# Attention in a two-layer hybrid network: probabilities scaled on GpSimd, latent attention in groups of two head columns

## The reference, cut to what matters

```
s = (q @ k.T) * scale                 # in C2: q,k of 64 columns, plus 32 rope columns whose k is shared by all heads
p = softmax(where(mask, s, NEG))      # B2: a window of 128 and a sink logit in the sum; D2: an added bias
o = p @ v
NSA: out = g0 * o_compressed + g1 * o_selected + g2 * o_window     # gates per token and head
```

## Time and profile before

| | us |
|---|---|
| median of 3 runs | 2278.95 |
| lowest, highest | 2278.51, 2280.58 |
| span of the profiled execution | 2275.0 |
| own time of the profiled execution | not listed apart from its span; the median is 3.95 above the span |
| TensorE busy in the span | 2199.9 |
| VectorE busy | 1246.9 |
| ScalarE busy | 1078.0 |
| GpSimd busy | 853.7 |

### The profile page before, as it was taken

The page is one execution under the profiler, slowest core; times in us unless marked ns, Lnnn a source line. Parts: engine busy times, 40 slices in busy tenths (PEclk is TensorE's granted clock), DMA queues, the critical chain, the costliest instruction groups (busy, mean ns, idle before and its releaser), DMA issues.

```text
span 2275.0 us, 33281 instructions
## 1 busy us (share of the span) xinstructions
PE 2199.9 (97%) x12130; PEld 1763.7 (78%) x12130; DVE 1246.9 (55%) x2614; ACT 1078.0 (47%) x2160; POOL 853.7 (38%) x665
## 2 busy tenths in 40 slices
PE   8999899999999999989999999999999999999997
PEld 6778667888866788668888888888767888888886
DVE  6997782499778446885552112234666655211222
ACT  6542484465247652685453223343566545322332
POOL 4333304443330343104255545554110425554553
PEclk9999899999999999999999999999999999999998
DMA  5334002332410233203233333343110323333331
GB/s 171 85 91 141 25 2 79 104 91 79 144 38 11 75 89 109 68 2 110 67 94 96 95 109 98 92 124 95 48 60 20 111 66 97 94 95 100 98 96 66
DMA packets 107186, 189.74 MB, mean 83 GB/s; under 512 B 12049, under 2 KB 22801, under 8 KB 106897
## 3 DMA queue, kind: packets, MB, share of 16 engines
q1 hardware_dynamic: 101136, 178.67, 27.3%
q10 hardware_dynamic: 5888, 8.95, 1.2%
HBM read 182.85 MB, written 2.10 MB: 81 GB/s over the span
## 4 chain that ended last, share of the span: by engine, by line
PE 85%; DVE 10%; issue 3%; ACT 2%; POOL 1%; DMA 0%; SPq 0%; DVEq 0%; ACTq 0%
PE bank L861 23%; PE bank L863 23%; PE bank L862 23%; PE bank L1090 3%; PE bank L1103 3%; PE bank L1076 2%; DVE temp L1933 1%; DVE bank L2053 1%; PE bank L868 1%; DVE temp L1965 1%; PE bank L1067 1%; PE bank L1070 1%; PE bank L931 1%; DVE temp L1967 1%; POOL w_lo L2212 1%
## 5 line engine op out<-in xcount | busy, mean ns | idle before, releaser
L2212 POOL TENSOR_TENSOR w_lo<-w_raw,w_hi 128x512 fp32r<-128x512 f32 (+3 forms) x618 | 824.7, 1341 | 1337.1 <-ACT w_hi L1226 1336.7
L861 PE MATMUL bank<-op_hi,w_hi 128*128 128x512 f32 x1840 | 734.4, 399 | 9.1 <-POOL w_lo L2212 4.4
L863 PE MATMUL bank<-op_hi,w_lo 128*128 128x512 f32 x1840 | 719.4, 391 | 0.0
L862 PE MATMUL bank<-op_lo,w_hi 128*128 128x512 f32 x1840 | 719.4, 391 | 0.0
L1226 ACT ACTIVATE w_hi<-w_raw 128x512 fp32r<-128x512 f32 (+2 forms) x634 | 385.4, 617 | 682.5 <-PE bank L863 678.8
L861 PEld LDWEIGHTS bank<-op_hi,w_hi 128*128 128x128 f32 x1840 | 347.1, 189 | 95.7 <-issue 15.3
L862 PEld LDWEIGHTS bank<-op_lo,w_hi 128*128 128x128 f32 x1840 | 347.6, 189 | 73.4 <-issue 4.1
L863 PEld LDWEIGHTS bank<-op_hi,w_lo 128*128 128x128 f32 x1840 | 347.1, 189 | 73.7
L1648 DVE TENSOR_TENSOR temp<-bank,rstd 128x512 f32<-128x512 f32 x151 | 104.4, 691 | 396.0 <-PE bank L863 378.2
L861 PE MATMUL bank<-side_hi,w_hi 128*128 128x512 f32 (+1 forms) x628 | 233.2, 371 | 2.5 <-DVE side_lo L1730 1.4
L863 PE MATMUL bank<-side_hi,w_lo 128*128 128x512 f32 (+1 forms) x628 | 230.9, 368 | 0.0
(11 more groups left out here) (269 smaller groups left out, 2256.3 us busy)
## 6 DMA issues: line engine op xcount, KB each, us to landing
w_raw<-in_weights SPq DMA_DIRECT2D x620, 256.0 KB, 2.7
w_raw<-in_weights SPq DMA_DIRECT2D x32, 192.0 KB, 2.3
temp<-temp SPq DMA_DIRECT2D x40, 64.0 KB, 2.0
x_t<-in_x SPq DMA_DIRECT2D x8, 256.0 KB, 5.4
conv_area<-in_mem ACTq DMA_DIRECT2D x2, 1024.0 KB, 5.5
out_y<-ybuf SPq DMA_DIRECT2D x8, 256.0 KB, 2.1
conv_area<-in_bias ACTq DMA_DIRECT2D x1, 1920.0 KB, 8.0
conv_area<-in_bias ACTq DMA_DIRECT2D x2, 960.0 KB, 4.9
```

The source lines that it names most:

```text
L861: pe.matmul(dst, w[0], m[0], start=start, stop=False)
L862: pe.matmul(dst, w[0], m[1], start=False, stop=False)
L863: return pe.matmul(dst, w[1], m[0], start=False, stop=stop)
L2212: pool.tensor_tensor(w_lo[:, j, 0:n], w_raw[:, p % RAW_RING, 0:n], w_hi[:, j, 0:n].bitcast(F32), ALU.subtract).then_inc(*mark("weights_spl ...
```

## The change

1. In all attention parts but X2, and not for NSA's compressed tiles, the multiply by the reciprocal moves from VectorE to a new loop `attend` on GpSimd. VectorE still computes the reciprocal. GpSimd's list of weight pieces becomes a `split_to` that is called between attention steps; the splits for the two strips behind an attention stand at the step that holds i = 10, and the layer norm's squares and adds stand at fixed steps.
2. C2 runs in groups of two pairs that belong to two neighbouring head columns. The four tiles' 32-row products stand together and use all four quarters of the array. Its turned copies are shared: ScalarE copies tiles 0 and 2 of a group, VectorE tiles 1 and 3. The third tile of a group is turned into the output bank of its group. Turning lags one group and values two.
3. Rings and banks: E 6 to 8, the fourth PT buffer is rstd, sums have 4 slots instead of 3; scores use four banks everywhere; the layer norm and the last gate strip use bank 7, so NSA has one output bank (6).
4. Output groups of A2, B2, C2 and D2 have four tiles instead of two.
5. Warm-up: none inside NSA, one more at the start of AB2. Gate strip chunks and drains are dealt out anew.

The diff, cut to its core:

```diff
-TURN_LAG = 2
-VALUE_LAG = 3
-OUT_LAG = 7
+PAIRS = {"NSA": 1, "AB2": 1, "D2": 1, "C2": 2, "X2": 1}
+TURN_LAG = {1: 2, 2: 1}
+VALUE_LAG = {1: 3, 2: 2}
+NEXT_SPLIT = 10
+VECTOR_COPIES = (1, 3)
-E_RING = 6
+E_RING = 8
-SCORES = (1, 2, 3)
-GATE_CHUNKS = (2, 1, 1, 4)
+SCORES = (1, 2, 3, 0)
+GATE_CHUNKS = (2, 2, 4)
-WARM_TURN = {"NSA": {30: 3}, "AB2": {0: 1}, "D2": {0: 2}, "C2": {0: 2}, "X2": {0: 2}}
+WARM_TURN = {"NSA": {}, "AB2": {0: 2}, "D2": {0: 2}, "C2": {0: 2}, "X2": {0: 2}}
...
-                                            size=2, pos=r, width=HD, y=ybuf[:, yc, qs], chunks=[yc], qs=slice(0, P), start=True, stop=True))
+                                            size=4, pos=2 * half + r, width=HD, y=y, chunks=chunks,
+                                            qs=slice(P * half, P * half + P), start=True, stop=True))
...
-                 "C2": ((0, 0), (0, 0, 0), (0, 1, 1), (1, 1, 1, 1, 0, 1)),
+                 "C2": ((0, 0), (0, 0, 0, 0, 1), (), (1, 1, 1, 1, 1)),
...
+                    t["out"], t["out_held"] = (6, at_group - 1) if step[1][0] == "NSA" else (6 + at_group % 2, at_group - 2)
+                    t["turn"] = 4 + n % 2
+                    if PAIRS[step[1][0]] == 2:
+                        third = t["out"] if step[1][0] != "NSA" else 7 if n >= LN_TILES else 4
+                        t["turn"] = (4, 5, third, 4 if third != 4 else 5)[n % 4]
...
+                    for pair in group:
+                        free_banks(pair)
+                        for x, y in parts:
+                            for t in pair:
+                                pe.matmul(score_bank(t), t["q"][x], t["k"][y], start=(x + y == 0), stop=False)
+                    for x, y in parts:
+                        for t in group[0] + group[1]:
+                            ins = pe.matmul(score_bank(t), t["more"][0][x], t["more"][1][y], start=False, stop=(x == 1))
...
                 def values(pair):
                     for t in pair:
-                        pe.wait_ge(*after("probs_copied", t["a"]))
-                        if t["first"] and t["g"] >= 2:
-                            pe.wait_ge(*after("outputs_taken", t["g"] - 2))
+                        pe.wait_ge(*copied(part, t["a"]))
+                        if t["first"] and t["out_held"] >= 0:
+                            pe.wait_ge(*after("outputs_taken", t["out_held"]))
+                        if t["first"] and t["size"] == 4:
+                            pe.wait_ge(*copied(part, t["a"] + 2))
...
+                    if scaled_by_pool(part, t):
+                        dve.reciprocal(total, total).then_inc(*mark("sums_inverted", a))
+                        return
...
+                def scaled(pair):
+                    t = pair[0]
+                    pool.wait_ge(*after("sums_inverted", pair[1]["a"]))
+                    total, _ = pair_sums(t)
+                    for r, t in enumerate(pair):
+                        e = E[t["a"] % E_RING][:, 0:t["nk"]]
+                        if t["gate"] is not None:
+                            ins = pool.tensor_scalar(e, e, total[:, r:r + 1], t["gate"], ALU.mult, ALU.mult)
+                        else:
+                            ins = pool.tensor_scalar(e, e, total[:, r:r + 1], None, ALU.mult)
+                        ins.then_inc(*mark("probs_scaled", t["a"]))
+
+                if part[0] == "NSA":
+                    norm_added(l)
+                for s in range(steps_of(part)):
+                    if part[0] == "NSA" and s == 14:
+                        norm_squares(l, 0, 2)
+                    for pair in in_group(groups, s - 1):
+                        if scaled_by_pool(part, pair[0]):
+                            scaled(pair)
+                    if NEXT_SPLIT in moments_of(part, s):
+                        split_to(last_of(FOLLOWS[part] + 1))
+                    if part[0] == "NSA" and s in (8, 9, 10, 11):
+                        norm_square(l, s - 8)
+                    if part[0] == "NSA" and s == 12:
+                        norm_squares(l, 0, 1)
+                    if part[0] == "NSA" and s == 13:
+                        norm_squares(l, 2, 3)
```

More of the change, by code:

```diff
@@ L600, in build @@
                     t["a"], t["g"] = at_tile, at_group
-                    banks = SCORES if step[1][0] == "NSA" and at_tile - ts[0]["a"] < LN_TILES else SCORES + (0,)
-                    t["bank"] = banks[(at_tile - ts[0]["a"]) % len(banks)]
+                    n = at_tile - ts[0]["a"]
+                    t["bank"] = SCORES[n % len(SCORES)]
                     t["held"] = held.get(t["bank"])
@@ L611, in build, with groups_of, lags_of, moments_of @@
                 ATT[step[1]] = ts
+        def groups_of(part):
+            n = 2 * PAIRS[part[0]]
+            return [[ATT[part][i + j:i + j + 2] for j in range(0, n, 2)] for i in range(0, len(ATT[part]), n)]
+        def lags_of(part):
+            return TURN_LAG[PAIRS[part[0]]], VALUE_LAG[PAIRS[part[0]]]
+        def moments_of(part, s):
+            n = 2 * PAIRS[part[0]]
+            return range(n * s, n * s + n)
+        def steps_of(part):
+            return len(groups_of(part)) + VALUE_LAG[PAIRS[part[0]]] + 2 - PAIRS[part[0]]
+        def in_group(groups, s):
+            return groups[s] if 0 <= s < len(groups) else []
         ENDS = 0
@@ L1152, in extra_stage @@
                     for i in range(NT):
[L1153 removed]
+                        ins = pe.matmul(bank[7][:, i:i + 1], u_conv[:, 0, PAD + P * i:PAD + P * i + P], C("ones")[:, 0:1], start=True, stop=True)
                     ins.then_inc(*mark(kind, l))
@@ L1427, in copy @@
                     act.wait_ge(*after("probs_turned", a))
+                    if part[0] == "NSA" and a == ts[PT_RING - 1]["a"]:
+                        act.wait_ge(*taken(LAST_GATE[part[1]]))
                     if a >= PT_RING:
@@ L1978, in output @@
                     else:
-                        ins = dve.tensor_copy(t["y"], o if w == HD else o.rearrange("p (r q) -> p r q", r=2))
+                        ins = dve.tensor_copy(t["y"], o if len(t["chunks"]) == 1 else o.rearrange("p (r q) -> p r q", r=2))
                     ins.then_inc(*mark("outputs_taken", g))
-                for i in range(len(ts) + OUT_LAG + 1):
-                    if i == OUT_LAG + 3:
+                groups = groups_of(part)
+                _, value_lag = lags_of(part)
@@ L1984, in attend @@
+                for s in range(steps_of(part)):
+                    if NEXT_SPLIT in moments_of(part, s):
                         split_to(last_of(FOLLOWS[part] + 1))
-                    if i < len(ts):
-                        maxed(ts[i])
-                    if NORM_LAG <= i < len(ts) + NORM_LAG and i % 2 == 1:
-                        normed(ts[i - NORM_LAG:i - NORM_LAG + 2])
-                    if OUT_LAG <= i < len(ts) + OUT_LAG and ts[i - OUT_LAG]["last"]:
-                        output(ts[i - OUT_LAG])
```

302 lines of the change are left out of this document (194 added, 108 removed).

## The result

The changed kernel takes 2340.21 us, the median of its runs (2338.89 to 2343.27), against 2279.76 of the kernel before on the same chip: 1.0271 times as long, interval 1.0256 to 1.0285. The forecast was 2274.4 with a range to 2292, so the result lies 48 us outside. The profiled span is 2341.5 us, 66.5 more than before. That execution is the slowest of the four (2343.27), so its span grew by more than the 60.5 us between the medians.

What follows compares the result with a forecast made beforehand. TensorE, busy 97% of the 2275.0 us span, was taken as the bound. The terms summed to -4.5, a span of 2270.5; adding 3.95 for the runs' median over the profiled span gave 2274.4 us, range 2257 to 2292.

Steps and rivals of the forecast that it cites:

- the price of the GpSimd multiply: Attention parts outside X2: 0.75 us for 512 columns, 0.5 for 384 or less, ends 0.61 and 1.04.
- rival (a): Every turning outside X2: GpSimd's multiply is long, 1.04 us, adding 24 us to the forecast, 2298; chance 0.16.
- The chain around it: A2 and D2: multiply waits on scores, maxima and GpSimd; two pairs take 4.46 + 2c against 5.90, almost no cost at 0.75.
- copy wait, A2 and D2: Values of each four-tile group wait for tile a+2's copy: 0.47 us a group, 8 groups each, +7.5.
- stall behind A2's splits: A2, step 5: pair 5's multiply queues behind GpSimd's four weight splits, stall 3.2 less 0.7 us, +2.5.
- one more blank product: AB2: one more warm-up matmul, half of a 1.98 us pair, +0.9.
- half B2: AB2's second half: VectorE relieved, then the GpSimd chain binds at 2.5 to 2.6 us a pair; -1 for 16 pairs.
- D2's bias: D2: long bias multiplications follow each other without VectorE's multiplies between; half of four waits goes, -1.1.
- C2, shared products: C2: four tiles' 32-row score products share all four array quarters, saving 0.90 us in 8 groups, -7.2.
- C2, start and splits: C2: later first turning costs +2.0, four splits behind group 1 delay group 2 by +1.3.
- NSA, two parts: NSA: second column falls from 31.1 to 26.4 us, columns one, three and four gain nothing; -9.4 for both parts.
- Rival (c): GpSimd's work stretches VectorE's remaining operations in NSA's compressed pairs, B2's sink sums and low halves; +8, 2282; chance 0.19.

Runs made afterwards that it cites:

- e1: Changed kernel with GpSimd's ungated multiply written as two operations (an extra times 1.0); 2288.17 us, 1.0046 of before.
- e7: Kernel before, with trial GpSimd multiplies in one- and two-operation forms ahead of A2's splits; 2280.86 us in one run.
- e5: Changed kernel with GpSimd multiplying in C2 alone, in two operations, no copy wait in A2, B2, D2, one blank product starting AB2; 2269.28 us, 0.9972.
- e10: As e9, but VectorE multiplies in A2, B2 and D2; 2267.66 us, 0.9957 of before.
- e9: As e6, with e8's silu order, VectorE multiplying tiles 26 and 27 of each NSA part, one blank product starting AB2; 2266.61 us, 0.9948.
- e2: Changed kernel with all multiplies back on VectorE, the rest of the change kept; 2281.53 us, 1.0025 of before.
- e4: As e1, without the wait for the copy of tile a+2 in A2, B2 and D2's groups of four; 2279.91 us in one run.
- e6: As e4, but GpSimd does A2's four weight splits one to a step, behind each step's multiplies; 2276.85 us in one run.
- e8: As e5, but NSA's second pair of silus stands behind the copies of the last turned pair; 2268.03 us, 0.9964.
- e3: Changed kernel with GpSimd multiplying in NSA alone, VectorE in AB2, D2 and C2; 2284.66 us in one run.

## Why the prediction was wrong

**The step that failed is the price of the GpSimd multiply.** "The new one has one wide input and two small scalars, so it is nearer the cast: I take c = 0.75 us for 512 columns ... and keep 0.61 and 1.04 as ends." That held for the multiply with the gate (0.82) and for neither end without it: c is 1.59. The mistake is one of reading the diff. It has two instructions, and the one without a gate has no second operation; they were priced as one, from rows of other instructions, and the rows at 0.61 and 1.04 were taken for bounds though neither is a tensor_scalar. For 384 columns or less 0.5 was taken, and 1.24 (384) and 1.01 (256) were measured. e1 and e7 show that the missing operation alone makes the difference. The range had a fault of its own: it ended at 2292, below the 2298 that rival (a) gave already for c = 1.04.

**The chain around it was right in A2, B2 and D2.** The forecast had for two pairs 4.46 + 2c, binding above c = 0.72. At c = 1.59 that is 7.64; measured in A2 behind the splits are 23.65 us for six pairs, 7.88 for two. D2 grew by 13.8 us, where eight times the 1.74 between 7.64 and 5.90 is 13.9. For B2 the forecast's sum with 1.24 and 1.01 gives an estimate of 6.1 for two pairs; measured are 38.2 us for twelve, 6.4 for two. Rival (a), the long multiply, was the case that came; its price was for c = 1.04. In NSA it did not apply, since the gated form is short.

**In C2 the long multiply cost 20.4 us** (84.8 against 64.4 in e1), a third of the loss, where rival (a) had 3 for c = 1.04. There the four multiplies of a group stand in one row, and TensorE waits for them before the next group. From the changed kernel's timeline:

```profile
1788.49 6.22 POOL L2347 TENSOR_SCALAR temp<-temp,small 128x512 f32<-128x512 f32 x4 [1.67 <-DVE small L2057]
```

The 6.22 and the 1.67 of waiting for the reciprocals make the 7.89 us from this group's scores to the next (1787.53 to 1795.42), for 6.33 in e5. By the same sum four multiplies at 1.04 would make 5.8, under 6.33, so the small price of (a) was no fault of the chain; c was beyond the end that it was made for.

The Trainium skill (GPSIMD Engine Reference, 4.1 Engine selection) says that one-input operations run near line rate on GpSimd: for the one-operation form no run here agrees, 1.59 us on GpSimd against VectorE's 0.88 for two such tiles. The 769 ns that the Trainium skill (GPSIMD Engine Reference, 3.1 Elementwise — side-by-side cycle accounting) gives for a tight loop of 512 elements is near the two-operation form (0.69 to 0.83) and half of the other. The advice of 4.1 to use VectorE for elementwise work holds here in AB2 and D2 (97.2 and 55.2 us in e10, 98.0 and 56.7 in e9), and not in C2, which is 3.1 us shorter with GpSimd's multiplies (e5 against e2).

**The other terms**, forecast and measured (with the two-operation form, where the long one hid them):

| term | forecast | measured |
|---|---|---|
| copy wait, A2 and D2 | +7.5 | 0.51 a group where it shows; taken out: -5.3 in AB2, -3.3 in D2 with VectorE's multiplies (e2 to e5, less the blank product), -1.5 and -3.1 with GpSimd's (e1 to e4) |
| stall behind A2's splits | +2.5, bound +6 with the lower clock | +4.2 (e6) |
| one more blank product | +0.9 | +0.9 (third to fourth pair 3.68 in e1, 2.82 before) |
| half B2 | -1 | +0.3 (52.4 in e4 and e5, 52.1 before) |
| D2's bias | -1.1 | +1.0 (pairs 8 to 15: 24.1 in e4, 23.1 before; 23.0 in e5) |
| C2, shared products | -7.2 | -10.7 if each group saves as the one measured |
| C2, start and splits | +3.3 | +3.0 |
| NSA, two parts | -9.4 | +2.9 (e1), +4.4 (after) |

The copy wait had its place and its size per group, but in AB2 most of it covered GpSimd's queue. The stall behind the splits came out at 3.9 us with the long multiply and 2.4 with the short one (e4), for 3.2, and what was kept as a bound, the lower clock behind it, did happen.

**NSA has the second wrong step.** "In all 26.4 for 31.1: -4.7 a part." The terms written there don't make this sum: 31.1 - 3.3 + 0.9 - 3 + 1.8 is 27.5. With VectorE's multiplies the column is near it, 27.2 us in e2's first part (28.6 in its second). With GpSimd multiplying, its queue behind the adds, which I had costed at 1.8 us, was itself the stall behind which the clock fell, to 0.52 in e1; the column came out at 31.4 in the changed kernel. The forecast removed one cause of a slow stretch and did not ask whether the 1.8 us of new waiting was another. "The tail waits for ScalarE's silus, unchanged" was wrong as well: from the last scores to the first part's end it was 14.2 us before and is 16.9 after. e8 shows part of the cause (the copies behind four silus) and leaves part open. The first column was 3.5 us shorter than before (23.2 for 26.7), at a clock of 1.00 for 0.87, where no gain was forecast. No run tested that; some of it is the execution, since e7, whose NSA is that of the kernel before, has 25.2 in its first part and 26.8 in its second.

Rival (c), that GpSimd's work stretches what VectorE keeps, has no run of its own, but the traces answer it. In the first NSA part the compressed pairs' sums take 416 ns in e1 and 413 in e2, their multiplies 288 in both; only the small multiply by the gates is longer, 344 for 163, which over its eight instructions is 1.4 us, and it was 301 before. The two operations on B2's sinks take 214 and 151 ns in e1 and before. The 8 us of its price did not come.

Four of the kernels beat both by a little: e5, e8, e9 and e10, with 0.9972, 0.9964, 0.9948 and 0.9957 of the time before, with intervals below 1 that overlap each other's. They keep the grouping of C2, which is the part of the change that pays.

## What to carry to other kernels

Price every new instruction in the form in which the diff writes it, the number of operations included; a row of another instruction of the same width is no bound, and where no row has the form, the range must say so. Where TensorE waits on a chain of equals, put the chain's two sides in a formula: it told the loss once the one price was known. And let the range of a forecast hold a slow stretch behind each new stall of TensorE: behind 1.8 us (e1, NSA) the column took 3.0 us more than in e2, behind 2.4 us (e4, AB2) the pair took 4.0 more than before, while the 2.3 us of e2 had none behind them.

## What the runs showed of the hardware that was not expected

GpSimd's tensor_scalar with one operation takes twice as long as with two, at 512 columns 1588 ns against 740 in the kernel and 1540 to 1590 against 690 to 770 side by side; at 384 columns it is 1243 against 588, and at 256 1012 against 570 (the changed kernel and e1). Whether that holds for operations other than the multiply was not tried, nor is it shown what makes it so. Executions with the same code ahead differ by up to 5.2 us in where the first NSA part begins (240.0 in e3, 245.2 in the changed kernel), and by 1.5 to 3 us in C2, by a stretch at a granted clock of 0.75 to 0.83 at its start.
